# Fewer slots for expert weights, and residual rows that stay in on-chip memory

## The chip, the core and the metric

The kernel runs on one core of a Trainium2 chip. The core has a matrix engine (TensorE, PE in the profile), a vector engine (VectorE, DVE), an activation engine (ScalarE, ACT), GpSimd (POOL) and a sync engine (SyncE, SP) that mainly issues DMAs; 16 DMA engines move data between DRAM and the on-chip memory. The metric is the device time of one execution in microseconds (us), as the median of several runs.

## What is computed

One layer of a decoder: adaLN modulation, a state-space group and an attention group side by side, an output projection, and then a mixture of experts with a shared expert. 1024 prompt tokens and 64 sample tokens are computed together, 1088 rows of 1024 numbers in float32. The change touches only the last part:

```python
def _block(x, c, past, ...):
    ...
    x = x + (gt1[:, None, :] * mix.astype(jnp.float32)).astype(x.dtype)   # residual rows: x1 in the kernel
    h = _norm_modulate(x, g_norm2, sh2, sc2)
    ff = _moe_ffn(h, w_router, router_bias, w_eg, w_eu, w_ed, w_sg, w_su, w_sd)
    x = x + (gt2[:, None, :] * ff.astype(jnp.float32)).astype(x.dtype)    # needs x1 again
    return x, state

def _moe_ffn(...):
    ...  # sigmoid scores, 4 of 8 groups, 6 of 64 experts for each row, weights w
    routed = _grouped_experts(x2, idx, w, w_eg, w_eu, w_ed)   # silu(x@wg) * (x@wu) @ wd, by expert
    shared = _swiglu(x2, w_sg, w_su, w_sd)
    return (routed + shared).reshape(Bn, L, Dm)
```

Each expert has a gate and an up matrix (1024 x 256) and a down matrix (256 x 1024), 1 MB each, and all 64 experts are read once.

## The kernel before

The program is written engine by engine: each engine has its own list of instructions, and semaphores tie them together. Nothing reorders them. The rows are held in nine tiles of 128 rows (the ninth has the 64 sample rows).

**On-chip memory.** Nearly all of it is one array, `arena`, in which each tensor has a fixed place that later tensors reuse. `x1`, the residual rows, lies at 39200 to 48416 (numbers of float32 in each partition). In the routed stage the weights of experts go into rings of slots: `gu_ring` (L337) has `GU_RING` = 6 slots of 2 MB from 4096 on, one for the gate and up matrices of an expert; `down_ring` (L338) has `DOWN_RING` = 5 slots of 1 MB, one at 28672 and four from 39200 on. These four lie over `x1`. That is why SP stores `x1` to a DRAM tensor `x1_tiles` first (`x_tiles` in the profile) and reads it back at the end.

**The shared stage** (about 1224 to 1334 us of the span). For each tile PE computes gate and up of the shared expert (L899, here of the next tile), ACT and POOL make the hidden rows, PE transposes them (L921) and multiplies by the down matrix (L927), ACT evicts the result into one of two buffers `y_buf` (L1944) and SP stores it to `moe_rows` in DRAM. Before an eviction into a buffer, ACT waits until the store from it two tiles ago has landed. The same SP queue holds, ahead of these stores: the rows of `h2`, the two stores of `x1` (L2240, L2241) and one DMA of 5376 KB that fills with zeros the part of `moe_rows` to which routed rows will be added (L2243). Beside this, DVE, PE and POOL compute the routing tables; `table_ready` tells SP that the experts are sorted.

**The routed stage** (about 1341 to 2117 us). The experts are sorted by how many rows they have, and a fixed plan (`ROUNDS`, with `NR` = 62 rounds, then a loop of two more) says which expert's rows stand in which quarter of a block of 128 rows: a large expert takes up to three rounds, and a round can hold the rest of one expert and all of another, or two small ones. For round b, PE does: gate/up of round b + 1 (L1011), transposes of the gathered rows of round b + 2 (L990), down of round b (L1022), transposes of hidden rows (L1029), an index product (L941). POOL gathers the rows of a round from `h2_rows` in DRAM and scatters the results, adding them to `moe_rows`.

**The loads of experts.** SP alone issues them, in a fixed order. `gu_sorted(k)` loads gate and up of the k-th expert of the order; from the seventh on it first waits until PE's gate/up of the last round of expert k - `GU_RING` is done. `down_sorted(k)` does the same for down, with `DOWN_RING`. In the order, gate/up k comes ahead of down k - 1, and an instruction that waits holds up all behind it:

```python
            for k in range(GU_RING, E):
                e_before, e_now = e_now, gu_sorted(k)
                down_sorted(k - 1, e_before)
```

The first loads are issued earlier: two experts' gate/up and one down as soon as `table_ready` is there, the others of the first `GU_RING` after the last shared tile is evicted. After these, and once the stores of shared rows and the zero fill have landed, SP adds one to `shared_stored`; ACT, DVE and POOL wait for it before round 0. The last round of each expert, in the plan's order, is 0, 1, 4, 4, 5, 5, 6, 7, 8, 9, 10, 10, 11, 12, 14, 14, 16, 16, 17, 17 for experts 0 to 19; expert 10 and 11 start in round 10, experts 18 and 19 in round 17, 38 and 39 in round 36, 58 and 59 in round 55.

**The end** (about 2124 us on). SP loads for each tile the shared rows, `x1` and the routed rows (L2306 to L2308); DVE adds the two (L1691), multiplies by the gate (L1692), adds to `x1` (L1693), and after the norm applies the modulation (L1703, L1704); SP stores the result.

Of the kernel before, what the change touches and what calls it, by code (L numbers as in the profile page):

```python
# [31 lines left out]
P = 128  # L32
D = 1024
# [31 lines left out]
MAXPAIR = (T * TOPK // P + E + 1) // 2  # L65
GU_RING = 6
DOWN_RING = 5
MAXBLK = 128
# [9 lines left out]
def rows(t):  # L78
    return P if t < 8 else NS
# [83 lines left out]
def hymba_program(nc, ap, out):  # L163

    ctx = ExitStack()
    with ctx:
# [6 lines left out]
        h2_dram = nc.dram_tensor("h2_rows", (T, D), F32, kind="Internal").ap()  # L173
        x1_dram = nc.dram_tensor("x1_tiles", (P, NT * D), F32, kind="Internal").ap()
        y_dram = nc.dram_tensor("moe_rows", (2 * (T + P), D), F32, kind="Internal").ap()
# [161 lines left out]
        gu_ring = arena(4096, GU_RING, 2, KD * FE)  # L337
        down_ring = [arena(28672, 2 * D)] + [arena(39200 + 2 * D * i, 2 * D) for i in range(DOWN_RING - 1)]  # L338
        x_rows = arena(0, 2, D)
# [727 lines left out]
        def _(dve):  # L1067
# [619 lines left out]
            for t in range(NT + 2):  # L1687
                if t < NT:
                    m, s_ = rows(t), int(t == 8)
                    dve.wait_ge(ld_y[t], 48)  # L1690
                    dlink(tt(y_rows[0:m, t, :], y_rows[0:m, t, :], y_rows2[t][0:m, :], ALU.add))  # L1691
                    dlink(tt(y_rows[0:m, t, :], y_rows[0:m, t, :], fin_rows[0:m, s_, :], ALU.mult))  # L1692
                    tt(x1[0:m, t, :], x1[0:m, t, :], y_rows[0:m, t, :], ALU.add).then_inc(x2_ready, 1)  # L1693
                if 1 <= t <= NT:
                    m = rows(t - 1)
                    dve.wait_ge(x2_sq, t)
                    ts(ssq[0:m, t - 1:t], ssq[0:m, t - 1:t], 1.0 / D, EPS, ALU.mult, ALU.add).then_inc(x_var, 1)
                if t >= 2:
                    i = t - 2
                    m, s_ = rows(i), int(i == 8)  # L1700
                    dve.wait_ge(x_std, NT + 3 + i)
                    dlink(dve.reciprocal(rstd[0:m, i:i + 1], rstd[0:m, i:i + 1]))
                    dlink(stt(x1[0:m, i, :], x1[0:m, i, :], rstd[0:m, i:i + 1], fin_rows[0:m, 2 + s_, :], ALU.mult, ALU.mult))  # L1703
                    tt(x1[0:m, i, :], x1[0:m, i, :], fin_rows[0:m, 4 + s_, :], ALU.add).then_inc(y_out_ready, 1)  # L1704
# [396 lines left out]
        def _(sp):  # L2101
# [137 lines left out]
            sp.sem_inc(rows_stored, 1)  # L2239
            dma(x1_dram[:, 0:8 * D], x1[:, 0:8, :].rearrange("p t d -> p (t d)")).then_inc(stored_h2[0], 16)  # L2240
            dma(x1_dram[0:NS, 8 * D:], x1[0:NS, 8, :]).then_inc(stored_h2[0], 16)  # L2241
            sp.wait_ge(routed, 1)
# [28 lines left out]
            slots.wait_full(sp, ("W", NT - 1, 1))  # L2271
            e_before = gu_sorted(0)
            e_now = gu_sorted(1)
            down_sorted(0, e_before)
            t = NT - 1
            sp.wait_ge(ys2_ready, NT)
            store(sp, y_dram[t * P:t * P + rows(t), :], y_buf[0:rows(t), t % 2, :], stored_ys[t % 2])
            sp.wait_ge(xn2_ready, NT)
            sp.wait_ge(stored_h2[0], 112)
            for k in range(2, GU_RING):  # L2280
                e_before, e_now = e_now, gu_sorted(k)
                down_sorted(k - 1, e_before)
            sp.wait_ge(stored_ys[0], 80)
# [21 lines left out]
            for t in range(NT):  # L2305
                dma(y_rows[0:rows(t), t, :], y_dram[t * P:t * P + rows(t), :]).then_inc(ld_y[t], 16)  # L2306
                dma(x1[0:rows(t), t, :], x1_dram[0:rows(t), t * D:(t + 1) * D]).then_inc(ld_y[t], 16)
                dma(y_rows2[t][0:rows(t), :], y_dram[T + P + t * P:T + P + t * P + rows(t), :]).then_inc(ld_y[t], 16)  # L2308
# [37 lines left out]
```

## Time and profile before

| | us |
|---|---|
| median of 3 runs (2194.28 to 2196.66) | 2195.11 |
| the profiled execution | 2194.29 |
| its span | 2192.5 |
| PE busy | 1926.2 |
| DVE busy | 871.3 |
| ACT busy | 470.6 |

The trace is of one execution, and all times in it count from the start of its span; what lies around the span is 1.8 us. A busy time is the time in which an engine ran an instruction; waits of the SP queue are time in which SP could issue no DMA. The DMA share is the mean busy share of the 16 DMA engines; it can come out a little above 1. The time from an issue to the landing runs from the start of the issuing instruction to the last update of the semaphore of that DMA.

### The profile page before, as it was taken

Reading aid. Unit: us, or ns where it says so; the run is one execution under the profiler, and the core shown is the slowest. Engines: PE = TensorE matmul, PEld = TensorE weight load, DVE = VectorE, ACT = ScalarE, POOL = GpSimd, SP = SyncE. Lnnn points to the kernel's source line nnn. Section 1 sums busy time; section 2 is a strip of 40 time slices with the busy share of each in tenths; the row PEclk is TensorE's granted clock in tenths of the full one; section 3 lists DMA queues with packets and bytes.
Section 4 is the critical chain, followed back from the end, with each engine's and each line's share of the span. In section 5 each row is a group of like instructions: output and inputs, shape, how many; then the busy total and the mean of one; then the engine's idle time right before and its main releaser. Section 6 shows DMA issues by size and latency. Waiting matters only on the chain.

```text
span 2192.5 us, 25291 instructions
## 1 busy us (share of the span) xinstructions
PE 1926.2 (88%) x8864; PEld 996.2 (45%) x8864; DVE 871.3 (40%) x2383; ACT 470.6 (21%) x899; POOL 217.6 (10%) x178
## 2 busy tenths in 40 slices
PE   3569899999988888887988888999999999999970
PEld 1146555555446666333546533444444444444440
DVE  4934631101335554222223623334344344443439
ACT  0122101210135454113023211111111111111122
POOL 0000000100000000030000001122221222212110
PEclk8679756899999998999997899999999999999985
DMA  7921001100112000444001628999999999999656
GB/s 282 366 78 44 22 1 51 70 0 1 48 36 79 1 1 20 131 159 144 0 1 48 201 74 332 350 380 375 374 383 371 381 376 360 358 374 383 215 166 237
DMA packets 99946, 398.64 MB, mean 182 GB/s; under 512 B 27055, under 2 KB 29779, under 8 KB 70108
## 3 DMA queue, kind: packets, MB, share of 16 engines
q1 hardware_dynamic: 80812, 327.81, 39.1%
q0 software_dynamic: 19008, 69.21, 12.0%
q8 instruction: 72, 1.18, 0.2%
q14 instruction: 54, 0.44, 0.1%
HBM read 333.88 MB, written 61.52 MB: 180 GB/s over the span
## 4 chain that ended last, share of the span: by engine, by line
PE 45%; issue 5%; DVE 3%; ACT 2%; DMA 1%; POOL 0%; POOLq 0%; SPq 0%; DVEq 0%; ACTq 0%
PE psum L1011 21%; PE psum L1022 10%; PE psum L865 5%; PE psum L990 3%; PE psum L1029 1%; PE psum L844 1%; PE psum L899 1%; PE psum L889 1%; PE psum L906 1%; PE psum L941 1%; DVE arena L1703 1%; DVE arena L1692 1%; DVE arena L1704 1%; DVE arena L1693 1%; DVE arena L1691 0%
## 5 line engine op out<-in xcount | busy, mean ns | idle before, releaser
L1011 PE MATMUL psum<-arena 128*32 128x512 f32 (+2 forms) x2016 | 464.3, 597 | 1.1 <-ACT arena L1957 1.1
L1011 PEld LDWEIGHTS psum<-arena 128*32 128x32 f32 (+2 forms) x2016 | 169.2, 139 | 242.1 <-issue 240.2
L1022 PE MATMUL psum<-arena,tail 128*32 128x512 f32 (+2 forms) x1000 | 231.6, 595 | 0.0
L1642 DVE TENSOR_TENSOR arena<-arena,psum 128x256 f32<-128x256 f32 x65 | 39.6, 610 | 339.9 <-ACT arena L1962 336.9
L2086 POOL DMA_INDIRECT moe_rows<-arena x64 | 101.7, 1589 | 575.6 <-DVE arena L1670 439.5
L1022 PEld LDWEIGHTS psum<-arena,tail 128*32 128x32 f32 (+2 forms) x1000 | 79.9, 138 | 105.3 <-issue 105.3
L713 PE MATMUL psum<-arena 128*128 128x512 f32 (+1 forms) x384 | 126.5, 493 | 0.0
L865 PE MATMUL psum<-arena 128*128 128x512 f32 (+1 forms) x288 | 124.3, 593 | 0.8 <-ACT arena L1888 0.5
L1962 ACT ACTIVATE arena<-psum 128x256 f32<-128x256 f32 x65 | 25.0, 384 | 444.9 <-PE psum L1011 444.9
L754 PE MATMUL psum<-arena 128*128 128x512 f32 (+2 forms) x192 | 86.8, 568 | 10.4 <-ACT arena L1818 10.4
L865 PEld LDWEIGHTS psum<-arena 128*128 128x128 f32 (+1 forms) x288 | 68.5, 239 | 55.3 <-issue 40.1
L713 PEld LDWEIGHTS psum<-arena 128*128 128x128 f32 x384 | 63.8, 193 | 62.6 <-issue 62.6
L573 PE MATMUL psum<-arena 128*32 128x512 f32 x256 | 50.5, 931 | 44.2 <-DMA arena<-in_w_ada 33.5
L1609 DVE TENSOR_TENSOR arena<-tail,arena 128x1152 bf16<-128x1152 f32 (+3 forms) x89 | 85.3, 984 | 0.0
L990 PEld LDWEIGHTS psum<-tail,arena 128*128 128x128 f32 x528 | 60.2, 142 | 49.7 <-issue 41.3
L1976 ACT ACTIVATE arena<-psum,arena 128x512 f32<-128x512 f32 x64 | 44.0, 687 | 159.0 <-PE psum L1022 148.9
L1670 DVE TENSOR_SCALAR arena<-psum,arena 128x512 f32<-128x512 f32 x64 | 48.0, 751 | 74.6 <-PE psum L1022 74.6
L763 PE MATMUL psum<-arena 128*128 128x64 f32 x576 | 77.0, 283 | 0.0
L1957 ACT ACTIVATE arena<-psum 128x1024 f32<-128x1024 f32 x66 | 67.6, 1024 | 42.5 <-PE psum L990 42.5
L990 PE MATMUL psum<-tail,arena 128*128 128x128 f32 x528 | 70.9, 278 | 6.4 <-DMA arena<-h_rows,arena 6.4
L763 PEld LDWEIGHTS psum<-arena 128*128 128x128 f32 x576 | 75.2, 206 | 0.0
L2074 POOL DMA_INDIRECT arena<-h_rows,arena x68 | 67.2, 988 | 48.1 <-DVE arena L1635 24.7
(481 smaller groups left out, 2440.6 us busy)
## 6 DMA issues: line engine op xcount, KB each, us to landing
arena<-in_w_exp_gate SPq DMA_DIRECT2D x66, 1024.0 KB, 20.1
arena<-in_w_exp_up SPq DMA_DIRECT2D x66, 1024.0 KB, 25.1
arena<-in_w_exp_down SPq DMA_DIRECT2D x66, 1024.0 KB, 22.5
arena<-in_w_ada SPq DMA_DIRECT2D x12, 2048.0 KB, 8.3
arena<-in_w_ada_final SPq DMA_DIRECT2D x4, 2048.0 KB, 8.8
arena<-in_cache_k SPq DMA_DIRECT2D x32, 256.0 KB, 3.9
arena<-in_cache_v SPq DMA_DIRECT2D x32, 256.0 KB, 3.0
arena<-moe_rows SPq DMA_DIRECT2D x16, 512.0 KB, 12.7
```

What stands on the lines that cost most here:

```text
L573: ins = pe.matmul(slot[2 + g % 2][32 * j:32 * (j + 1), :], cs_t[:, k, :], ada_w[:, n % 2, k % KPER, j * 512:(j + 1) * 512], start=(k == 0) ...
L713: ins = pe.matmul(slot[b][:, 0:c1 - c0], w_q[:, k, w * DA + j * P:w * DA + (j + 1) * P], hT[:, k, c0:c1], start=(k == 0), stop=(k == KD - 1))
L754: ins = pe.matmul(slot[it % 2][:, c0:c1], qT[:, h, i * P:(i + 1) * P], kT[:, h // 2, c0:c1], start=True, stop=True)
L763: ins = pe.matmul(slot[4 + it % 2][:, 0:DH], pt[:, it % 2, j * P:(j + 1) * P], v[:, j, h * DH:(h + 1) * DH], start=(j == 0), stop=(j == i))
L865: ins = pe.matmul(slot[half][0:rows(t), n * 512:(n + 1) * 512], lhs, w_out[:, half * KA + k, n * 512:(n + 1) * 512], start=(k == 0), stop= ...
L990: ins = pe.transpose(slot[0][:, k * P:(k + 1) * P], x_rows[:, par, k * P:(k + 1) * P], ident)
L1011: ins = pe.matmul(slot[2 + par][lo:hi, :].rearrange("p (u n) -> p u n", u=2), xTs[:, par, k, lo:hi], gu, start=(k == 0), stop=(k == KD - 1))
L1022: ins = pe.matmul(slot[1][lo:hi, n * 512:(n + 1) * 512], hTs[:, k, lo:hi], down_ring[at][:, k * D + n * 512:k * D + (n + 1) * 512], start= ...
L1609: ins = tt(onehot[:, par, :, lo * LANE:hi * LANE], iota_row[:, lo * LANE:hi * LANE].unsqueeze(1).to_broadcast([P, NT, w]), blk_rank[:, par ...
L1957: f(xTs[:, par].rearrange("p k c -> p (k c)"), slot[0], ACT.Copy).then_inc(xt_copied, 1)
L2074: pool.indirect_dma_start(x_rows[:, par, :], None, h2_dram, bass.IndirectOffsetOnAxis(ap=g_idx[:, par:par + 1], axis=0)).then_inc(gathered ...
L2086: pool.indirect_dma_start(y_dram, bass.IndirectOffsetOnAxis(ap=s_idx[:, par:par + 1], axis=0), y_buf[:, par, :], None, compute_op=ALU.add) ...
```

## The change

The rings get 5 and 3 slots. All of them now lie between 4096 and 30720 of `arena`: five gate/up slots up to 24576, and three down slots behind them. `x1` is overlaid by nothing from then on, so the DRAM tensor, its two stores and its nine loads are gone, and so is the wait for the stores. Of the early loads only gate/up and down of the first expert remain ahead of the last shared store, since the next slot lies over the shared weights. The order of the loads behind stays gate/up k, down k - 1.

```diff
@@ -63,8 +63,8 @@
 NEG = -1e30
 MAGIC = 12582912.0
 MAXPAIR = (T * TOPK // P + E + 1) // 2
-GU_RING = 6
-DOWN_RING = 5
+GU_RING = 5
+DOWN_RING = 3
 MAXBLK = 128
 LANE = 32
 CAPS = (10, 9, 9, 8, 8, 7) + (6,) * 5 + (5,) * 11 + (4,) * 8 + (3,) * 16 + (2,) * 14 + (1,) * 4
@@ -171,7 +171,6 @@
         tail_t = ctx.enter_context(nc.sbuf_tensor("tail", [P, 4280], F32))
         psum = ctx.enter_context(nc.psum_tensor("psum", [P, 8, 512], F32))
         h2_dram = nc.dram_tensor("h2_rows", (T, D), F32, kind="Internal").ap()
-        x1_dram = nc.dram_tensor("x1_tiles", (P, NT * D), F32, kind="Internal").ap()
         y_dram = nc.dram_tensor("moe_rows", (2 * (T + P), D), F32, kind="Internal").ap()
 
         def arena(at, *shape, dt=F32, parts=P):
@@ -335,7 +334,7 @@
         sh_gu = arena(13056, KD, 2 * FE)
         sh_d = arena(17152, 2, D)
         gu_ring = arena(4096, GU_RING, 2, KD * FE)
-        down_ring = [arena(28672, 2 * D)] + [arena(39200 + 2 * D * i, 2 * D) for i in range(DOWN_RING - 1)]
+        down_ring = [arena(4096 + 2 * D * (11 + i), 2 * D) for i in (1, 0)] + [arena(4096 + 2 * D * 10, 2 * D)]
         x_rows = arena(0, 2, D)
         xTs = arena(2048, 2, KD, P)
         y_buf = arena(31776, 2, D)
@@ -1687,7 +1686,7 @@
             for t in range(NT + 2):
                 if t < NT:
                     m, s_ = rows(t), int(t == 8)
-                    dve.wait_ge(ld_y[t], 48)
+                    dve.wait_ge(ld_y[t], 32)
                     dlink(tt(y_rows[0:m, t, :], y_rows[0:m, t, :], y_rows2[t][0:m, :], ALU.add))
                     dlink(tt(y_rows[0:m, t, :], y_rows[0:m, t, :], fin_rows[0:m, s_, :], ALU.mult))
                     tt(x1[0:m, t, :], x1[0:m, t, :], y_rows[0:m, t, :], ALU.add).then_inc(x2_ready, 1)
@@ -2237,8 +2236,6 @@
             sp.wait_ge(stored_h2[0], 80)
             sp.wait_ge(stored_h2[1], 64)
             sp.sem_inc(rows_stored, 1)
-            dma(x1_dram[:, 0:8 * D], x1[:, 0:8, :].rearrange("p t d -> p (t d)")).then_inc(stored_h2[0], 16)
-            dma(x1_dram[0:NS, 8 * D:], x1[0:NS, 8, :]).then_inc(stored_h2[0], 16)
             sp.wait_ge(routed, 1)
             dma(y_dram[T:, :].rearrange("(a p) d -> p a d", p=E), y_zero[0:E, :].unsqueeze(1).to_broadcast([E, (T + 2 * P) // E, D])).then_inc(stored_h2[1], 16)
             for t in range(NT - 1):
@@ -2269,17 +2266,16 @@
 
             sp.wait_ge(table_ready, 1)
             slots.wait_full(sp, ("W", NT - 1, 1))
-            e_before = gu_sorted(0)
-            e_now = gu_sorted(1)
-            down_sorted(0, e_before)
+            e_now = gu_sorted(0)
+            down_sorted(0, e_now)
             t = NT - 1
             sp.wait_ge(ys2_ready, NT)
             store(sp, y_dram[t * P:t * P + rows(t), :], y_buf[0:rows(t), t % 2, :], stored_ys[t % 2])
             sp.wait_ge(xn2_ready, NT)
-            sp.wait_ge(stored_h2[0], 112)
-            for k in range(2, GU_RING):
+            for k in range(1, GU_RING):
                 e_before, e_now = e_now, gu_sorted(k)
-                down_sorted(k - 1, e_before)
+                if k > 1:
+                    down_sorted(k - 1, e_before)
             sp.wait_ge(stored_ys[0], 80)
             sp.wait_ge(stored_ys[1], 64)
             sp.wait_ge(stored_h2[1], 80)
@@ -2304,7 +2300,6 @@
             sp.wait_ge(routed_done, 1)
             for t in range(NT):
                 dma(y_rows[0:rows(t), t, :], y_dram[t * P:t * P + rows(t), :]).then_inc(ld_y[t], 16)
-                dma(x1[0:rows(t), t, :], x1_dram[0:rows(t), t * D:(t + 1) * D]).then_inc(ld_y[t], 16)
                 dma(y_rows2[t][0:rows(t), :], y_dram[T + P + t * P:T + P + t * P + rows(t), :]).then_inc(ld_y[t], 16)
             for t in range(NT):
                 sp.wait_ge(y_out_ready, t + 1)
```

On SP, the queue of DMAs, the part from the stores of `h2` rows to the first expert loads stood so before (`x_tiles` and `moe_rows` are the DRAM tensors, `in_w_exp_gate`, `in_w_exp_up` and `in_w_exp_down` the weights):

```order
L518 DMA h_rows<-arena 64x1024 [waits h2_ready]
L2240 DMA x_tiles<-arena 128x8192 [waits stored_h20,stored_h21]
L2241 DMA x_tiles<-arena 64x1024
L2243 DMA moe_rows<-arena 64x21x1024 [waits routed]
L518 DMA moe_rows<-arena 128x1024 [waits ys2_ready] x8
L2259 TENSOR_LOAD arena [waits slot_filled1,table_ready]
```

And now:

```order
L517 DMA h_rows<-arena 64x1024 [waits h2_ready]
L2240 DMA moe_rows<-arena 64x21x1024 [waits stored_h20,stored_h21,routed]
L517 DMA moe_rows<-arena 128x1024 [waits ys2_ready] x8
L2256 TENSOR_LOAD arena [waits slot_filled1,table_ready]
L2256 ISA x2
```

The two stores of `x1` have gone from ahead of the zero fill, and so the fill and the shared stores each stand two DMAs earlier.

Later on the same queue, before, the place of the first wait for a slot: the loads of gate/up 5 and down 4, then those of gate/up 6 and down 5.

```order
L2253 DMA arena<-in_w_exp_up 128x2048
L2256 DMA arena<-in_w_exp_down 128x2048
L2259 TENSOR_LOAD arena [waits stored_h21,stored_ys0,stored_ys1]
L2259 ISA x2
L2253 ISA [waits gu_done]
L2253 DMA arena<-in_w_exp_gate 128x2048
L2253 DMA arena<-in_w_exp_up 128x2048
L2256 DMA arena<-in_w_exp_down 128x2048 [waits down_done]
```

And now, the loads of gate/up 4 and down 3, then those of gate/up 5 and down 4:

```order
L2250 DMA arena<-in_w_exp_up 128x2048
L2253 DMA arena<-in_w_exp_down 128x2048 [waits down_done]
L2256 TENSOR_LOAD arena [waits stored_h21,stored_ys0,stored_ys1]
L2256 ISA x2
L2250 ISA [waits gu_done]
L2250 DMA arena<-in_w_exp_gate 128x2048
L2250 DMA arena<-in_w_exp_up 128x2048
L2253 DMA arena<-in_w_exp_down 128x2048 [waits down_done]
```

The first wait for `down_done` now stands ahead of the waits for the stores and thus ahead of `shared_stored`, which is raised right after them; before it came behind.

## Rows read from the trace of the kernel before

**Rows 1.** The page, part 1: busy time, share of span, instructions by engine.
```profile
PE 1926.2 (88%) x8864; PEld 996.2 (45%) x8864; DVE 871.3 (40%) x2383; ACT 470.6 (21%) x899; POOL 217.6 (10%) x178
```

**Rows 2.** Table of stretches: length, busy time by engine, clock granted, DMA share, GB/s.
```profile
1265.80:1276.00 10.20, 4.73 (x7) 2.14 (x8) 0.00 (x0) 2.18 (x4) 0.73 (x1) 0.50 0.31 127
1267.00:1327.00 60.00, 52.67 (x190) 23.12 (x190) 18.56 (x81) 12.38 (x23) 3.69 (x5) 0.93 0.12 49
1346.00:1366.00 20.00, 19.53 (x75) 9.82 (x74) 7.53 (x26) 3.44 (x5) 0.94 (x1) 0.96 1.01 426
1413.00:2035.00 622.00, 622.00 (x3585) 270.12 (x3582) 255.31 (x937) 109.42 (x157) 133.78 (x104) 1.00 1.02 372
2132.00:2190.00 58.00, 0.00 (x0) 0.00 (x0) 55.93 (x63) 12.68 (x28) 0.00 (x0) 0.51 0.67 260
```

**Rows 3.** Waits of the SP queue from 1200 us on: total us, times, longest.
```profile
SPq L2256 <- PE psum L1022: 423.4, 35, 16.3
```

**Rows 4.** DMA issues of 1226.6 and 1227.5: KB, us to landing; SP's row.
```profile
x_tiles<-arena SPq DMA_DIRECT2D x1, 4096.0 KB, 11.9
...
moe_rows<-arena SPq DMA_DIRECT2D x1, 5376.0 KB, 39.1
...
1227.50 1.35 SPq L2243 DMA_DIRECT2D moe_rows<-arena  x1
```

**Rows 5.** Timeline of ACT, evictions of shared rows: start, us, idle before and releaser.
```profile
1244.87 1.02 ACT L1944 ACTIVATE arena<-psum 128x1024 f32<-128x1024 f32 x1 [3.79 <-PE psum L927]
...
1267.94 1.02 ACT L1944 ACTIVATE arena<-psum 128x1024 f32<-128x1024 f32 x1 [15.61 <-DMA moe_rows<-arena]
```

**Rows 6.** Timeline of PE, fourth and fifth shared tile.
```profile
1252.39 3.70 PE L927 MATMUL psum<-arena,tail 128*128 128x512 f32 x8 [0.47 <-ACT tail L1940]
1255.92 7.03 PE L899 MATMUL psum<-arena 128*128 128x512 f32 x16
...
1270.79 0.69 PE L921 MATMUL psum<-tail,arena 128*128 128x128 f32 x2 [7.84 <-POOL arena L2063]
1271.95 5.69 PE L927 MATMUL psum<-arena,tail 128*128 128x512 f32 x8 [0.47 <-ACT tail L1940]
```

**Rows 7.** Timeline of DVE at the end; DMA issues of 2124.3 and 2124.8 us.
```profile
2131.77 1.23 DVE L1691 TENSOR_TENSOR arena<-arena 128x1024 f32<-128x1024 f32 x1 [11.54 <-DMA arena<-moe_rows]
...
arena<-x_tiles SPq DMA_DIRECT2D x1, 512.0 KB, 5.4
...
arena<-moe_rows SPq DMA_DIRECT2D x1, 512.0 KB, 6.9
```

**Rows 8.** Timelines of SP, ACT and PE around round 0 of the loop.
```profile
1365.37 0.33 SPq L2256 DMA_DIRECT2D arena<-in_w_exp_down  x1
...
1361.94 1.02 ACT L1957 ACTIVATE arena<-psum 128x1024 f32<-128x1024 f32 x1 [0.44 <-PE psum L990]
...
1353.90 7.13 PE L1011 MATMUL psum<-arena 128*128 128x512 f32 x16 [0.24 <-ACT arena L1957]
...
1365.62 7.11 PE L1011 MATMUL psum<-arena 128*128 128x512 f32 x16
```

**Rows 9.** Timeline of PE: down of rounds 4, 5; gate/up of 10, 17.
```profile
1409.02 3.64 PE L1022 MATMUL psum<-arena,tail 128*32 128x512 f32 x32
...
1421.01 3.64 PE L1022 MATMUL psum<-arena,tail 128*32 128x512 f32 x32
...
1460.28 7.07 PE L1011 MATMUL psum<-arena 128*32 128x512 f32 x64
...
1543.34 7.07 PE L1011 MATMUL psum<-arena 128*32 128x512 f32 x64
```

**Rows 10.** DMA issues of 1412.7, 1426.2 and 1498.7: KB, us to landing.
```profile
arena<-in_w_exp_down SPq DMA_DIRECT2D x1, 1024.0 KB, 5.7
...
arena<-in_w_exp_up SPq DMA_DIRECT2D x1, 1024.0 KB, 24.0
...
arena<-in_w_exp_up SPq DMA_DIRECT2D x1, 1024.0 KB, 39.2
```

## The prediction

> **What bounds the kernel now.** I read the page first: PE is busy 88% of the span, DVE 40% [rows 1]. Then the table of stretches, because an average says nothing of where a change acts. From 1413 to 2035 us PE is busy 622.00 of 622.00 us at the full clock (2.4 GHz), and in the same stretch the DMA share is 1.02, that is full, at 372 GB/s [rows 2]. So in the routed stage PE sets the pace and the DMA engines keep up with nothing to spare: the weights arrive just as fast as PE eats them, and what keeps PE from feeling it is the stock of weights in the slots. The waits of the SP queue say how that stock is kept: it stood 423.4 us for a down slot to come free [rows 3]. SP wants to run ahead and the slots hold it. The change takes slots away, so the question is how much stock each round needs. The other two places that the change touches are the shared stage, where PE once stands idle, and the end, where DVE waits for its first rows; both are read below.
>
> The profiled execution took 2194.29 us, 1.8 us more than its span of 2192.5; the median of the three runs is 2195.11, 0.8 above it. I sum on 2194.29 and add the 0.8 at the end. About 0.2% (4.4 us) is what a measurement of this kernel can tell from no change.
>
> **Part 1, the store of the residual rows goes.** At 1226.6 SP issues 4 MB of x1, and at 1227.50 the zero fill of `moe_rows` behind it; they land 11.9 and 39.1 us after their issues, at 1238.5 and 1266.6 [rows 4]. The fill alone thus takes 28.1 us. The first store of shared rows is behind the fill, and ACT waits for it 15.61 us until 1267.94 [rows 5]. ACT's lateness reaches PE: PE ends the gate/up of the next tile at 1255.92 + 7.03 = 1262.95, and starts the next transposes at 1270.79 after 7.84 us of idle time. The matmuls behind it take 5.69 us where the same eight took 3.70 one tile earlier [rows 6], since after that idle time the granted clock is 0.50 (1.2 GHz) [rows 2]. Cost of the wait: 7.84 + 1.99 = 9.8 us. Without the x1 store the fill lands at about 1226.6 + 28.1 = 1255, the store behind it by 1257; a plain tile later than ACT's eviction at 1244.87, that is at about 1256, ACT wants it. Its remaining wait of 1 us ends before PE is done at 1262.95. So the wait goes: **-9.8 us** (bounds -8 and -10). Next late is nothing on DMA's side: the stores of the following tiles find empty queues (DMA share 0.12 from 1267 on [rows 2]).
>
> **Part 2, the reload at the end goes.** DVE's first add waits for the three loads of tile 0 until 2131.77 [rows 7]. Those of x1 and of the second half of `moe_rows` were issued 0.5 us apart and land 5.4 and 6.9 us after their issues, so without the x1 load the last lands about one such transfer earlier, 1.5 to 2.0 us. Afterwards DVE is busy, 55.93 of 58 us [rows 2], either way. **-1.7 us.** The other 8 x1 loads are hidden behind DVE now and give nothing.
>
> **Part 3, the signal that opens the loop.** Before, SP issued five down loads without any wait and then set `shared_stored`. Now the fourth down load waits for the down matmuls of round 0, and the signal stands behind it on SP; ACT, DVE and POOL all wait for that signal before their first round. In the trace the sixth down load waits for those matmuls and is issued at 1365.37, ACT evicts the turned rows of round 2 from 1361.94 for 1.02 us and PE starts that gate/up at 1365.62 [rows 8]. In the changed kernel ACT can start its gate only after 1365.37 + 0.33 and some semaphore steps, at about 1366.3, its eviction 0.8 us later ends at 1368.1 and PE starts at about 1368.5: **+2.9 us**, once (bounds 0 and 4). The second gate/up load, which now waits for the last shared rows, is wanted only at 1353.90, after the first gate/up [rows 8]; I take no cost for it (0 to 2).
>
> **Part 4, the stock of weights.** SP's order is gate/up k+1, down k, gate/up k+2, down k+1. A down load k now waits until expert k-3 is done (k-5 before), and each gate/up load stands behind the down load ahead of it on the queue. Expert 2 has three rounds and is done with the down matmuls of round 4, at 1409.02 + 3.64 = 1412.66 [rows 9]. In the trace the load that waits for this is down 7, issued at 1412.7, and it lands 5.7 us later, which is what one load costs in a short queue [rows 10]. After the change it is down 5. So from this moment the same queue is behind by down 5, gate/up 7, down 6, gate/up 8: 6 MB.
>
> What a MB costs in the full queue: the up load of expert 11 is issued at 1426.2 and lands 24.0 us later, at 1450.2; that of expert 19 at 1498.7 + 39.2 = 1537.9 [rows 10]. Between lie 8 experts of 3 MB: 87.7 / 24 = 3.65 us each. 6 MB are then 21.9 us. With weights alone in the queues, at 426 GB/s from 1346 to 1366 [rows 2], a MB takes 1.049 / 426 = 2.46 us, and 6 MB 14.8. How much the stock covers: expert 11 is wanted at 1460.28, 10.1 us after it landed; expert 19 at 1543.34, 5.4 us after [rows 9]. So PE loses 21.9 - 10.1 = 11.8 us by expert 11 and 21.9 - 5.4 = 16.5 us by expert 19, at the price of the full queue; 14.8 - 5.4 = 9.4 at that of weights alone. While PE stands, fewer scatters and gathers run beside the weights, so I take a value between, nearer the full queue's: **+13 us**.
>
> Later the stock can't grow again as it did. From the rounds, ten gate/up loads (experts 7, 19, 29, 31, 39, 41, 49, 51, 59, 61) get their slot only one round before PE wants them; with five down slots none did. In that round one down and two gate/up loads, 3 MB, must land. A round is 1421.01 - 1409.02 = 12.0 us [rows 9]. The fixed part of a load is 5.7 - 2.46 = 3.2 us; 3 MB take 3 x 3.65 + 3.2 = 14.2 us in the full queue (2.2 us late) and 3 x 2.46 + 3.2 = 10.6 alone (in time). Two of the ten are in the 13 us; the other eight cost 0 to 17.6 us, and as a scatter and a gather run in every round I take 1.5 each: **+12 us**.
>
> A rule of the Trainium skill speaks against this loss: "Trainium Kernel Development and Optimization", section Best Practices, says to double-buffer so that DMA overlaps with compute, and three slots are more than two. By that rule part 4 would be 0 and the sum -6.6 in place of +18.4; with the DMA share at 1.02 [rows 2] there is nothing left to overlap with, so I take it for the first rival only. For the transfers, "DMA: Bandwidth & Descriptors" (section Anatomy of one DMA, the path of DMAs that GpSimd issues) has a fit of 2.0 us plus bytes / 436 GB/s; by it, as an estimate, 3 MB in a row are 9.2 us and the eight loads cost nothing.
>
> **Clock.** After an idle time of 7.84 us the clock fell and cost 2 us (part 1). The waits of rounds 10, 17 and of two or three later ones may be of 4 us and more, so up to 10 us; but where the queue is the limit, a slower PE only waits less for the next load. **+2 us** (0 to 8).
>
> **Sum:** -9.8 - 1.7 + 2.9 + 13 + 12 + 2 = +18.4. 2194.29 + 18.4 + 0.8 = 2213.5 us.
>
> **Rivals.** (A) *Faster.* The loss of part 4 stays hidden, and the gains of parts 1 and 2 come through with the cost of part 3: 2195.1 - 9.8 - 1.7 + 2.9 = 2186.5. For it: both loads that I followed landed 5.4 us or more before use, and PE never waited. It decides if the queue catches up 6 MB within the 47.6 us from 1412.66 to 1460.28, which needs a MB at under 3.0 us there (15 MB and the fixed part), against the 3.65 seen. I give it 0.11. It is also what double-buffering as the Trainium skill has it (page and section above) would lead one to expect. (B) *No change.* Part 4 stays at its low end, 9.4 and nothing later, and the clock costs nothing: 2195.1 - 8.6 + 9.4 = 2195.9, within the noise: 0.09. (C) *Worse.* Six down loads (5, 19, 29, 39, 49, 59) get their slot only when the round before their own is done, and are wanted at 1421.01 - 1412.66 = 8.4 us after [rows 9]; alone one takes 5.7, behind 3 MB of backlog 4 x 3.65 + 3.2 = 17.8, that is 9.4 us late. If the backlog is there each time, four of them beyond what is counted add 38: 2251. Against it: the load ahead of them was issued two rounds earlier. 0.06. That the change doesn't do what it says I exclude: the order of the built program has no row of `x_tiles` left.
>
> **How the numbers follow.** The forecast, slower, has 0.74. Its own range is part 4 from 12 to 34, the rest from -9 to +3 (part 3 at 4 and the clock at 8): 2198 to 2232. The 8-in-10 range goes down to 2195, so that B is in it, and up to 2238, where the clock's 8 us are in it too: A below and C above are left out, 0.17. Faster by more than 0.2%: case A, 0.11. Same: case B, 0.09. Slower: the forecast and C, 0.80.
>
> **What would show it.** Part 1: no idle time of PE before the transposes of the fourth shared tile, and the routed stage starting some 10 us earlier. Part 2: DVE's first add 1.5 to 2 us sooner after SP's first load. Part 3: PE's third gate/up of the loop waits 3 us. Part 4: PE rows of gate/up (`L1011`'s line) with idle time ended by DMA from the weights, the longest at rounds 10 and 17, then small ones at 27, 29, 36, 38, 46, 48, 55, 57, and none on the down side; the DMA share below 1 near 1400. I am wrong if PE waits for no weights, or waits for the down weights, or if the shared stage still stands at the fill.

## The result, and the profile after

The changed kernel takes **2227.61 us** (median of four runs, 2224.8 to 2229.44), the kernel before 2195.89 beside it (four runs, 2194.28 to 2197.43). The ratio is 1.0143, 95% interval 1.0126 to 1.0161: 31.7 us slower. The forecast was slower, 2213.5, with a range of 2195 to 2238. The profiled execution has a span of 2227.7 us, 35.2 more than before.

The page of the changed kernel first: busy time by engine (as in [rows 1]), the chain of work that ended last by engine and by line (cut by the page itself), and the group of the gate/up matmuls, now `L1010` (lines of the changed kernel are one lower there).

```profile
PE 1935.7 (87%) x8864; PEld 995.0 (45%) x8864; DVE 870.8 (39%) x2383; ACT 469.7 (21%) x899; POOL 217.3 (10%) x178
...
PE 37%; DMA 9%; issue 5%; DVE 3%; ACT 2%; SPq 1%; POOL 0%; POOLq 0%; DVEq 0%; ACTq 0%
PE psum L1010 17%; DMA arena<-in_w_exp_up 8%; PE psum L1021 8%; PE psum L864 5%; PE psum L989 2%; PE psum L898 1%; PE psum L888 1%; PE psum L905 1%; DVE arena L1702 1%; PE psum L892 1%; DVE arena L1691 0%; DVE arena L1692 0%; DVE arena L170
...
L1010 PE MATMUL psum<-arena 128*32 128x512 f32 (+2 forms) x2016 | 474.8, 608 | 32.3 <-DMA arena<-in_w_exp_up 31.2
```

PE now stands 32.3 us ahead of the gate/up matmuls, 31.2 of them for the up half of the weights, and this transfer holds 8% of the chain. The same group in the kernel before, with 1.1 us:

```profile
L1011 PE MATMUL psum<-arena 128*32 128x512 f32 (+2 forms) x2016 | 464.3, 597 | 1.1 <-ACT arena L1957 1.1
```

Next the table of stretches, with the columns of [rows 2]: the stretch that [rows 2] has, and one ahead of the loop's longest wait.

```profile
1413.00:2035.00 622.00, 591.74 (x3397) 258.09 (x3397) 240.49 (x884) 102.59 (x147) 126.00 (x99) 0.98 0.98 353
...
1380.00:1410.00 30.00, 30.00 (x237) 12.48 (x236) 12.85 (x41) 6.28 (x9) 5.14 (x4) 1.00 0.58 143
```

The second of these stretches in the kernel before:

```profile
1380.00:1410.00 30.00, 30.00 (x213) 12.76 (x215) 10.55 (x36) 5.45 (x8) 6.46 (x6) 1.00 1.03 375
```

From 1413 to 2035 PE was busy all of the time before [rows 2] and is idle for 30 us of it now; the DMA share went from 1.02 to 0.98. So PE and DMA both lost. From 1380 to 1410 the DMA engines are 0.58 busy in place of 1.03, while PE works on without a pause. The waits of the SP queue say why (total, times, longest), against 423.4 us, 35 times, at most 16.3 in [rows 3]:

```profile
SPq L2253 <- PE psum L1021: 635.7, 36, 33.7
```

`L2253` is the down load. The view has no wait of `L2250`, the gate/up load, for its own slot: when SP gets to a gate/up load, the slot has always been free for some time. The profile before had 120.0 us of such waits in 19 pieces, so there SP did stand at the gate/up slots now and then:

```profile
SPq L2253 <- PE psum L1011: 120.0, 19, 18.2
```

PE's timeline, the gate/up matmuls that had to wait, with those of an undisturbed round ahead; the bracket is the idle time before:

```profile
1660.60 7.07 PE L1010 MATMUL psum<-arena 128*32 128x512 f32 x64
...
1466.93 8.40 PE L1010 MATMUL psum<-arena 128*32 128x512 f32 x64 [8.83 <-DMA arena<-in_w_exp_up]
...
1676.44 9.47 PE L1010 MATMUL psum<-arena 128*64 128x512 f32 x32 [3.88 <-DMA arena<-in_w_exp_up]
...
1792.03 9.70 PE L1010 MATMUL psum<-arena 128*64 128x512 f32 x32 [3.87 <-DMA arena<-in_w_exp_up]
```

And the stretches around the start of round 10's matmuls:

```profile
1463.00:1469.50 6.50, 2.56 (x13) 0.71 (x17) 0.00 (x0) 0.00 (x0) 0.00 (x0) 0.50 1.04 340
1470.00:1475.00 5.00, 5.00 (x52) 1.46 (x44) 0.00 (x0) 0.00 (x0) 0.00 (x0) 1.00 1.02 423
```

These are rounds 10, 27 and 36. Each of these three waits is paid twice: the idle time, and then matmuls of 8.4 to 9.7 us in place of 7.1, since the granted clock is 0.50 (1.2 GHz) behind the wait and 1.00 (2.4 GHz) again some us later. Most of the shorter waits are paid once: behind 1.7 us at rounds 7 and 17 and 2.5 us at round 46 the matmuls take 7.1.

A late load need not have idle DMA engines ahead of it. Ahead of round 27 they are full, though SP issues nothing from 1641.2 to 1660.1:

```profile
1642.00:1661.00 19.00, 19.00 (x118) 8.63 (x114) 8.24 (x27) 4.19 (x6) 2.57 (x2) 1.00 1.02 351
```

**Where the 35.2 us are.** I cut the span at PE's first transpose of the normalised rows (`L906` before, `L905` now; 18.7 us ahead of the shared expert's first gate/up), at the start of the first gate/up of round 0 (1341.94 before, 1334.35 now) and at the end of the last down matmuls of all 64 rounds (2115.72 and 2152.75).

| stretch | before, us | after, us | difference |
|---|---|---|---|
| ahead of the first cut (noise) | 1152.4 | 1154.9 | +2.5 |
| norm and shared stage, to the gate/up of round 0 | 189.6 | 179.4 | -10.1 |
| routed stage | 773.8 | 818.4 | +44.6 |
| end | 76.8 | 75.0 | -1.8 |

In the routed stage, summed by round over the time from the end of the down matmuls to the next gate/up beyond its usual 0.35 us: round 2 1.8; rounds 7, 10 and 17 12.6; fourteen late rounds in all 34.7, of which 20.3 from round 27 on. Five slow gate/ups behind them (rounds 2, 10, 27, 36 and 55, at 8.4 to 9.7 against 7.1) add 10.5. 34.7 + 10.5 = 45.2, against 44.6 seen. Counted from start to start of the gate/ups, which needs no usual value, the waits are 34.1, and the sum is 44.6.

### The profile page after: what moved, and what is told of

It reads as the page before. It is cut to its first block, busy times and chain, and to the rows that moved or that the text cites. A ratio compares the mean times of both kernels' runs of the same rounds, so it can differ in the third digit from the quotient of the medians.

```text
span 2227.7 us, 25279 instructions
## 1 busy us (share of the span) xinstructions
PE 1935.7 (87%) x8864; PEld 995.0 (45%) x8864; DVE 870.8 (39%) x2383; ACT 469.7 (21%) x899; POOL 217.3 (10%) x178
## 3 DMA queue, kind: packets, MB, share of 16 engines
q0 software_dynamic: 19008, 69.21, 11.9%
## 4 chain that ended last, share of the span: by engine, by line
PE 37%; DMA 9%; issue 5%; DVE 3%; ACT 2%; SPq 1%; POOL 0%; POOLq 0%; DVEq 0%; ACTq 0%
PE psum L1010 17%; DMA arena<-in_w_exp_up 8%; PE psum L1021 8%; PE psum L864 5%; PE psum L989 2%; PE psum L898 1%; PE psum L888 1%; PE psum L905 1%; DVE arena L1702 1%; PE psum L892 1%; DVE arena L1691 0%; DVE arena L1692 0%; DVE arena L1703 0%; PE psum L843 0%; DVE arena L1690 0%
## 5 line engine op out<-in xcount | busy, mean ns | idle before, releaser
L1010 PE MATMUL psum<-arena 128*32 128x512 f32 (+2 forms) x2016 | 474.8, 608 | 32.3 <-DMA arena<-in_w_exp_up 31.2
L1010 PEld LDWEIGHTS psum<-arena 128*32 128x32 f32 (+2 forms) x2016 | 175.3, 141 | 278.5 <-issue 276.9
```

The lines of the kernel that those rows point to most:

```text
L1010: ins = pe.matmul(slot[2 + par][lo:hi, :].rearrange("p (u n) -> p u n", u=2), xTs[:, par, k, lo:hi], gu, start=(k == 0), stop=(k == KD - 1))
```

## The experiments

Two things were in question. My forecast said "stock", without saying of which slots. The trace puts the waits at the gate/up weights. So: do five gate/up slots cost the time, or three down slots? And if the down slots, is it the storage, or the order of the loads on SP's one queue?

**Three down slots alone, in the kernel before.**

```diff
-DOWN_RING = 5
+DOWN_RING = 3
-            for k in range(2, GU_RING):
+            for k in range(2, 4):
...
-            for k in range(GU_RING, E):
+            for k in range(4, E):
```

> The kernel before (six gate/up slots, residual rows still stored and read back) with three down slots alone; shared_stored is raised right before the first down load that has to wait, two loads earlier than in the kernel before. Theory of the down slots (the gate/up load of expert k+1 stands on SP's queue behind the down load of k, which waits for the down slot of k-3, so that its own free slot helps nothing): gate/up late at rounds 10, 27, 36, 46 and 55 as in the changed kernel, some 30 us late in all and 10 us more of slow clock, 2195.9 + 30 to 42 = 2226 to 2238 us. Rival of the gate/up slots (the waits stand at the gate/up weights, so the fifth slot in place of the sixth costs the time): no late load, 2194 to 2198 us. Middle, both: 2205 to 2220 us.

2237.18 us, ratio 1.0179 (1.0150 to 1.0208). Its gate/up group and SP's wait, as above:

```profile
L1011 PE MATMUL psum<-arena 128*32 128x512 f32 (+2 forms) x2016 | 470.1, 605 | 32.0 <-DMA arena<-in_w_exp_up 30.9
...
SPq L2256 <- PE psum L1022: 624.3, 36, 33.6
```

The expectation of the down slots is met, in time and in the late rounds. With six gate/up slots and as much idle time for late weights as in the changed kernel (32.0 and 32.3 us), the sixth gate/up slot helps nothing. The loss is that of the down slots, though PE waits for gate/up weights.

**Five gate/up slots alone, in the kernel before.**

```diff
-GU_RING = 6
+GU_RING = 5
...
-        gu_ring = arena(4096, GU_RING, 2, KD * FE)
+        gu_ring = arena(8192, GU_RING, 2, KD * FE)
```

> The kernel before with five gate/up slots alone (five down slots, residual rows stored and read back as before). Theory of the down slots: no gate/up waits for its weights by more than 1 us in the routed stage, 2194 to 2199 us. Rival of the gate/up slots: late loads at rounds 10, 27, 36 and 55 and 2220 us or more.

2198.03 us, ratio 0.9997 (0.9978 to 1.0016). PE is busy throughout, as before the change:

```profile
1413.00:2035.00 622.00, 622.00 (x3602) 269.37 (x3601) 255.34 (x936) 109.59 (x157) 133.56 (x104) 1.00 1.02 373
```

The rival of the gate/up slots falls: taken alone, the sixth slot is worth nothing that can be measured.

**The same bytes, given out as four gate/up and five down slots, in the changed kernel.**

```diff
-GU_RING = 5
-DOWN_RING = 3
+GU_RING = 4
+DOWN_RING = 5
...
-        gu_ring = arena(4096, GU_RING, 2, KD * FE)
-        down_ring = [arena(4096 + 2 * D * (11 + i), 2 * D) for i in (1, 0)] + [arena(4096 + 2 * D * 10, 2 * D)]
+        gu_ring = arena(12288, GU_RING, 2, KD * FE)
+        down_ring = [arena(28672, 2 * D)] + [arena(4096 + 2 * D * i, 2 * D) for i in range(4)]
```

> The changed kernel with its 13 half slots given out as four gate/up and five down slots in place of five and three: the same bytes on chip, one gate/up slot less. Theory of the down slots: the late loads of rounds 27 to 57 are gone and those of rounds 10 and 17 halve, because the down load no longer stands in front of the gate/up load; 13 us of lateness at most is left of 34.7, so 2227.6 - 20 to - 38 = 2190 to 2208 us. Rival of the gate/up slots: one slot less makes every wait longer, 2235 to 2270 us. Rival that all the stock counts alike (13 half slots is what matters): 2222 to 2233 us.

2192.91 us, ratio 0.9975 (0.9961 to 0.9988). One wait for weights is left, at round 10, and SP now waits for gate/up slots and hardly for down slots:

```profile
PE psum L1010 <- DMA arena<-in_w_exp_up: 3.7, 1, 3.7
...
SPq L2250 <- PE psum L1010: 519.3, 35, 33.2
SPq L2253 <- PE psum L1021: 50.0, 12, 11.2
```

It is not the total of the stock that counts: the same 13 half slots, shared out another way, are better than five and three by 1.7% of the time, 37 us.

**The same slots, another order on SP.** The down load of expert k-2, in place of k-1, stands behind the gate/up load of k.

```diff
...
-                e_before, e_now = e_now, gu_sorted(k)
-                down_sorted(k - 1, e_before)
-            down_sorted(E - 1, e_now)
+                es.append(gu_sorted(k))
+                down_sorted(k - 2, es[k - 2])
+            for k in (E - 2, E - 1):
+                down_sorted(k, es[k])
```

> The changed kernel with another order on SP's queue and the same slots: the down load of expert k-2 stands behind the gate/up load of k, in place of that of k-1 (shared_stored is raised before the first down load that waits, since only three of them come before it now). Theory of the order (a gate/up load whose slot is free waits behind a down load whose slot is not): the gate/up waits go, a few down loads come some us late (the one at round 10 most), 10 us or less of lateness in place of 34.7 and little slow clock, 2227.6 - 25 to - 38 = 2190 to 2203 us. Rival of the storage (three down slots hold too little, in whatever order): the lateness moves to the down weights, 2220 to 2235 us. Rival of the gate/up slots: the order on the queue counts little, 2222 to 2230 us.

2198.81 us, ratio 1.0001 (0.9985 to 1.0016): 1.4% of the time by the order (and the earlier signal that comes with it, worth nothing measurable by itself, below; in the traces the routed stage is 784.9 us here and 811.9 with the early signal alone). One example of what the order does is expert 29. First the changed kernel, PE's and SP's timelines: the gate/up that frees the slot, the down matmuls that the load ahead of it on SP waits for, and the loads.

```profile
1636.72 7.07 PE L1010 MATMUL psum<-arena 128*32 128x512 f32 x64
...
1656.46 3.64 PE L1021 MATMUL psum<-arena,tail 128*32 128x512 f32 x32
...
1660.16 0.33 SPq L2253 DMA_DIRECT2D arena<-in_w_exp_down  x1
1661.24 0.34 SPq L2250 DMA_DIRECT2D arena<-in_w_exp_gate  x1
1661.68 0.43 SPq L2250 DMA_DIRECT2D arena<-in_w_exp_up  x1
```

The same in this kernel, with the gate/up that uses the weights at the end:

```profile
1630.92 7.08 PE L1010 MATMUL psum<-arena 128*32 128x512 f32 x64
...
1638.20 0.34 SPq L2250 DMA_DIRECT2D arena<-in_w_exp_gate  x1
...
1666.69 7.09 PE L1010 MATMUL psum<-arena 128*64 128x512 f32 x32
```

In the changed kernel the slot is free at 1636.72 + 7.07 = 1643.8, but the load ahead of it on SP waits for the down matmuls that end at 1656.46 + 3.64 = 1660.1, and the gate/up load follows 1.1 us later: 17.4 us lost with a free slot. Here it is issued 0.2 us after its slot is free (1638.0). Over all gate/up loads that need a slot to come free (59, in the kernel before 58), the mean from the slot's release to the issue is 19.6 us in the changed kernel (none under 14.7), 9.5 in this one and 9.2 in the kernel before.

The example is the rule. In the change's order gate/up k stands behind down k-2, and that load waits, with three slots, for the down matmuls of expert k-5: each of the 59 loads is issued 1.1 to 4.4 us after these end. With six gate/up slots it stands behind the same matmuls, which is why the sixth slot helped nothing. The other order, or a fourth down slot, puts the matmuls of expert k-6 there. The loss goes with the time from the issue to the use, and not with the time that a slot stands free (in the mean 31.3 us with three down slots alone, at about the same loss, and 2.4 with five gate/up slots alone, against 9.2 before, at none). The shortest time from the issue of an up load to PE's want of it is 33.9 us in the kernel before and 27.9 with five gate/up slots alone, 22.2 in this run, 16.2 with four and five slots, and 10.6 in the changed kernel and with three down slots alone.

What stays here is 8.0 us of waits for down weights, since a down load still waits for the expert three before it, the longest at round 10:

```profile
PE psum L1021 <- DMA arena<-in_w_exp_down: 8.0, 3, 6.1
PE psum L1010 <- DMA arena<-in_w_exp_up: 0.7, 1, 0.7
```

**Four down slots, in either order.** A fourth slot in two halves, where the zeros and the dead tables of the routing lay; first with the order of the last experiment, then with that of the changed kernel (there with the early signal of the experiment after next). The diff is cut to the ring; the down load and the down matmuls address the slot in two halves.

```diff
...
-DOWN_RING = 3
+DOWN_RING = 4
-        down_ring = [arena(4096 + 2 * D * (11 + i), 2 * D) for i in (1, 0)] + [arena(4096 + 2 * D * 10, 2 * D)]
+        down_ring = [arena(4096 + 2 * D * (12 - i), 2, D) for i in range(3)] + [arena(30720, 2, 6496)[:, :, 0:D]]
...
```

> The changed kernel with the order of the run before (the down load of expert k-2 behind the gate/up load of k) and a fourth down slot, in two halves that lie where the zeros of the zero fill and the dead tables of the routing were. Theory: the order and the fourth slot leave no load late by more than 1.5 us, the routed stage is as long as before the change (774 to 778 us), the gains of the shared stage and of the end stay: 8 to 11.5 us less than before, ratio 0.9948 to 0.9963. Rival (the queue is full, and any lost slot costs): down of round 10 and the like still late by 3 us or more and a slow gate/up behind it, ratio 0.998 to 1.003. Rival (loads in two halves are slower): the down loads take longer by 1 us or more each, ratio 1.0 or more.

> The changed kernel in its own order (the down load of expert k-1 behind the gate/up load of k) with the fourth down slot in two halves and shared_stored raised before the down load of expert 3; with the run before it, it makes a square of three or four down slots in either order. Theory (one more down slot lets the down load at the head of SP's queue go a round or so earlier, and so takes most of what the order costs): one or two gate/up loads late, at round 10 or 17, by 3 to 7 us in all with a slow gate/up behind them, none at rounds 27 to 58; 4 us less than before to 2 us more, ratio 0.998 to 1.001. Rival (the fourth slot is worth little without the other order): late loads at rounds 27 to 58 as in the changed kernel, ratio 1.008 to 1.014.

2187.55 us, ratio 0.9964 (0.9948 to 0.9980), and 2192.66 us, ratio 0.9986 (0.9973 to 1.0000). All that PE waited for weights in the one and in the other:

```profile
PE psum L1021 <- DMA arena<-in_w_exp_down: 3.6, 1, 3.6
```

```profile
PE psum L1010 <- DMA arena<-in_w_exp_up: 5.6, 2, 4.3
```

The square of ratios: three down slots 1.0143 in the change's order and 1.0001 in the other, four 0.9986 and 0.9964. Either the order or one more down slot takes most of the loss away; together they add little. In the traces the routed stage is 44.6 us longer than before with neither, 11.1 with the other order, 7.1 with the fourth slot and 4.1 with both. The second expectation was met (two late gate/ups, rounds 10 and 17). The first was not quite: the down of round 17 was late by 3.6 us where I had asked for under 1.5, with slow matmuls behind it as its first rival has them (5.34 us in place of 3.64), and the ratio lies just outside what I gave, and below the rivals'. The one with both is faster than the kernel before, by 7.9 us.

**The gains alone: the kernel before without the store and the reload of the residual rows** (this part of the computation is left out: the last addition reads weights in place of these rows).

```diff
...
-            dma(x1_dram[:, 0:8 * D], x1[:, 0:8, :].rearrange("p t d -> p (t d)")).then_inc(stored_h2[0], 16)
-            dma(x1_dram[0:NS, 8 * D:], x1[0:NS, 8, :]).then_inc(stored_h2[0], 16)
...
-                dma(x1[0:rows(t), t, :], x1_dram[0:rows(t), t * D:(t + 1) * D]).then_inc(ld_y[t], 16)
```

> The kernel before with six gate/up and five down slots, without the store of the residual rows and without reading them back; the down slots lie over these rows as before, so the last addition reads weights in their place and y_prompt and y_sample carry that: this part of the computation is left out. It is the first two terms of the forecast alone. Theory: 9.8 us less in the shared stage and 1.7 us less at the end, ratio 0.9948 (11.5 of 2195), no late weights. Rival (the store is hidden, and its place is taken by the zero fill's transfer or by the second load): ratio 0.998 to 1.000.

2184.74 us, ratio 0.9952 (0.9931 to 0.9974): 10.5 us by the ratio, of the 11.5 forecast; the interval is 5.7 to 15.2 us. The rival (hidden store) falls.

**The signal earlier, in the changed kernel.**

```diff
-            for k in range(1, GU_RING):
+            for k in range(1, GU_RING - 1):
...
+            e_before, e_now = e_now, gu_sorted(GU_RING - 1)
             sp.wait_ge(stored_ys[0], 80)
             sp.wait_ge(stored_ys[1], 64)
             sp.wait_ge(stored_h2[1], 80)
             sp.sem_inc(shared_stored, 1)
+            down_sorted(GU_RING - 2, e_before)
```

> The changed kernel with shared_stored raised before the down load of expert 3 in place of behind it. Theory (the signal stood behind that load's wait for down of round 0): the gate/up of round 2 is no longer late (1.8 us) and runs at full clock (8.8 to 7.1 us), ScalarE's and VectorE's waits for that signal (12.0 and 7.8 us) shrink to a few; 2 to 3.5 us less, ratio 1.0130 to 1.0135 to the kernel before in place of 1.0143; the later late loads stay. Rival (the time is given back at the next late load, since the rounds run ahead of the queue that sets them): round 2 is on time, but the lateness at rounds 7 and 10 grows by as much, ratio 1.014 to 1.015.

2226.61 us, ratio 1.0144 (1.0120 to 1.0167): no difference to the changed kernel that this measurement can tell. ACT's third gate, in the changed kernel and in this one, and PE's gate/up of round 2 in both:

```profile
1358.20 0.38 ACT L1961 ACTIVATE arena<-psum 128x256 f32<-128x256 f32 x1 [12.02 <-SPq L2282]
...
1359.84 8.81 PE L1010 MATMUL psum<-arena 128*128 128x512 f32 x16
```

```profile
1352.15 0.38 ACT L1961 ACTIVATE arena<-psum 128x256 f32<-128x256 f32 x1 [7.27 <-PE psum L1010]
...
1356.66 7.11 PE L1010 MATMUL psum<-arena 128*128 128x512 f32 x16
```

The wait and the slow clock are gone, as the theory has it, and PE's wait for weights is 29.5 us in all (31.2 in the changed kernel). The ratio is where the rival put it. But its sign did not come: rounds 7 and 10 are late by 10.7 us together in both kernels. Whether those 3.5 us reach the end is **not settled**: the interval is 10 us wide.

**Half of each down load left out, in the changed kernel** (2.5 MB an expert in place of 3; the second half of each down matrix is left out).

```diff
-                dma(down_ring[q], ed[bass.ds(e, 1)].rearrange("a p n -> (a p) n")).then_inc(ld_down[q], 16)
+                dma(down_ring[q][:, 0:D], ed[bass.ds(e, 1)].rearrange("a p n -> (a p) n")[:, 0:D]).then_inc(ld_down[q], 16)
```

> The changed kernel with half of each down load left out (the second 1024 of 2048 numbers of each partition are never read from DRAM, so the experts' outputs are wrong): the same slots, waits and order, but 2.5 MB in place of 3 MB for an expert. Theory (where an expert has one round only, 3 MB do not fit in 12 us of a full queue, so bytes set the late loads behind the release): the lateness of rounds 27 to 58 falls from 20.3 to under 8 us, that of rounds 10 and 17 from 10.7 to under 4 us, and the time by 18 to 35 us, ratio 0.998 to 1.006. Rival (the order on the queue alone sets them: a gate/up load is issued 17 us after its slot is free, whatever the bytes): lateness of 16 us or more at rounds 27 to 58, ratio 1.009 to 1.014.

2201.47 us, ratio 1.0024 (1.0005 to 1.0043). The stretch of [rows 2], and PE's waits:

```profile
1413.00:2035.00 622.00, 607.71 (x3506) 266.97 (x3504) 247.43 (x906) 106.60 (x153) 128.95 (x101) 1.00 0.93 317
```

```profile
PE psum L1010 <- DMA arena<-in_w_exp_up: 15.4, 11, 2.4
...
SPq L2253 <- PE psum L1021: 599.8, 36, 33.7
```

The time fits the theory of the bytes, the lateness neither: the rounds from 27 on are late by 11.9 us together (20.3 with all bytes; I had set under 8 for the one, 16 or more for the other), rounds 10 and 17 by 3.1 (10.7). So both act. With the DMA share at 0.93 and SP waiting as long as before, eight rounds from 27 on are still late by 1.1 to 2.4 us each: that I put down to the order, since their loads are issued a round before use whatever they weigh (at least 10.6 us before PE wants them, as in the changed kernel). The rest, 8.4 us there and 7.6 at rounds 10 and 17, is bytes. It is more than one trace differs from another: from start to start of the gate/ups the rounds from 27 on are late by 11.2 us here, and by 19.8, 19.3 and 17.4 in the changed kernel, with three down slots alone and with the early signal.

## Why the forecast was right in sign and 14 us short

- **Part 1 (forecast -9.8):** -10.1 in the trace. PE's transposes, `L921` in [rows 6], have no idle time any more, and ACT's wait of 15.61 us [rows 5] is 5.13, hidden from PE as forecast (at most other tiles ACT waits 3.79 for PE itself). The timelines of PE and ACT:

```profile
1265.26 0.38 PE L920 MATMUL psum<-tail,arena 128*128 128x128 f32 x2
...
1259.93 1.02 ACT L1943 ACTIVATE arena<-psum 128x1024 f32<-128x1024 f32 x1 [5.13 <-DMA moe_rows<-arena]
```

- **Part 2 (-1.7):** -1.8. DVE's first add starts 5.7 us after SP's first load, against 7.9 before (the add in [rows 7]); first the load before, then the load and the add now:

```profile
2123.90 0.33 SPq L2306 DMA_DIRECT2D arena<-moe_rows  x1
...
2161.26 0.33 SPq L2302 DMA_DIRECT2D arena<-moe_rows  x1
...
2166.98 1.23 DVE L1690 TENSOR_TENSOR arena<-arena 128x1024 f32<-128x1024 f32 x1 [9.73 <-ACTq L1990]
```

- **Part 3 (+2.9):** the place was right, ACT's bracket above names the signal; 1.8 us late and 1.7 of slow clock, 3.5. I had not priced the clock there.
- **Part 4, first term (+13):** rounds 7, 10 and 17 are 12.6 us late. The missing queue time is directly to be seen: 30 us at 0.58 in place of 1.03 from 1380 to 1410 are 13.5 us in which the DMA engines had nothing, from 1392.1 on with two gate/up slots free. I called it a stock that is 6 MB short; it is idle DMA time behind a load that may not go yet. That 13 came so near is in part luck: I chose it between two prices, 9.4 and 16.5. And I had named rounds 10 and 17 as the longest waits: round 17 has 1.7 us, and rounds 27, 36 and 55 have 3.9 to 4.4.
- **Part 4, second term (+12):** this step is mis-sized; 20.3 us, beyond my own bound of 17.6 (1.1 of them at rounds 39 and 58, which I had not named). The ten loads that I counted are the right ones: their up halves are issued 10.6 to 11.0 us before PE wants them, those before 34.7 to 57.8. The sum let each of the eight rounds start with an empty queue and 3 MB. Take expert 29: its up load, issued at 1661.68, lands 14.6 us later, at 1676.3, and PE wanted it at about 1672.5. But the up load of expert 28, issued at 1640.74, takes 24.3 us and is still on its way until 1665.0. The DMA issues of 1661.68 and 1640.74, KB and us to landing:

```profile
arena<-in_w_exp_up SPq DMA_DIRECT2D x1, 1024.0 KB, 14.6
...
arena<-in_w_exp_up SPq DMA_DIRECT2D x1, 1024.0 KB, 24.3
```

So 3 MB and what was left of an older load went through in 1676.3 - 1660.2 = 16.1 us, where I had 14.2 at most; the other price that I named for 3 MB in a row, 9.2, fell further short. The late rounds come in pairs two rounds apart (27 and 29, 36 and 38, 46 and 48, 55 and 57); the first of each pair carry 15.0 of the 20.3 us, the other six rounds about 1 us each. With less in the queue (half the down bytes) the eight become alike, at 1.1 to 2.4 us: the 1.5 that I took for each is what the order costs without a backlog, as far as that run shows it.
- **Clock (+2):** the step that failed. I let a slow PE be made up for, because "a slower PE only waits less for the next load". It cost 10.5 us, 8.8 without the 1.7 of round 2, over my bound of 8 either way, and the books close only if all of it stays (45.2 summed, 44.6 seen). The next load here waits for a slot that the slow matmuls themselves free, so it moves back with them; this reason fits the waits of SP, and no run tests it alone.
- **The rivals:** A fell by the first late row, and B by the time and the late rows after round 10. C fell as well: no down load was late. I put that down to the gate/up load that stands behind each and is late first. That the down loads come late instead shows only with the other order (6.1 us at round 10).
- **The rule of double-buffering** ("Trainium Kernel Development and Optimization" in the Trainium skill, Best Practices), by which part 4 would have been 0: with three slots the trace has 635.7 us of SP's waits and 31.2 of PE's. A count of slots above two did not decide it; the same three slots make the routed stage 44.6 us longer or 11.1, by the order of the loads behind them.

Terms against trace: -10.1 - 1.8 + 3.5 + 12.6 + 20.3 + 8.8 (the clock without round 2's) = +33.3 where I had +18.4; with 2.5 us of noise ahead of the change that is 35.8, and the span grew by 35.2.

## What to carry to other kernels

When one queue issues the loads of two rings, its order is worth as much as its storage: look for loads that are issued long after their own slot is free and shortly before their use, since the ring that PE waits for need not be the one that is short. The sign is that the waits of the queue are all at the other ring's line; here the late loads went out 10.6 to 11.0 us before their use, where it was 34.7 or more. A DMA share below 1 need not come with it: it was 0.58 ahead of round 10, but 1.02 ahead of round 27. Before taking slots away, follow which release each load stands behind, and put ahead on the queue what is released first; and price the slow clock behind the longer waits. Here those of 3.9 to 8.8 us had it, at 1.3 to 2.6 us each, and all of it stayed in the sum.

## What the runs showed that I had not expected

The shared stage comes in two lengths in kernels that do the same in it. Of the kernels without the store of x1, three took 174.2 to 174.7 us and four more, beside the changed kernel, 178.8 to 179.6 (cut as in the table). The difference arises ahead of the routing; the same 65 us from the first cut on, with four gate/up and five down slots (of the longer kind) and with the other order and three down slots (of the shorter), columns as above:

```profile
1163.40:1228.40 65.00, 53.50 (x286) 44.63 (x287) 23.49 (x75) 25.37 (x24) 0.00 (x0) 0.79 0.14 57
```

```profile
1162.50:1227.50 65.00, 52.04 (x318) 42.84 (x319) 25.66 (x81) 27.46 (x26) 0.00 (x0) 0.87 0.16 65
```

The mean granted clock is 0.79 in the one and 0.87 in the other. Both have idle times of 1.3 to 1.7 us ahead of each tile from 39 us on; in the changed kernel, which is of the longer kind, the clock falls to 0.50 four times between 41 and 69 us, in the one of the shorter kind once between 39 and 67. Why the one or the other comes, no run tells. The kernel before is of the longer kind too, so the -10.1 of part 1 compares like with like; whether a kernel with the store ever has the shorter, its three traces (187.1 to 189.6 us) do not tell:

```profile
1152.40:1217.40 65.00, 53.36 (x286) 44.47 (x286) 23.45 (x75) 25.32 (x24) 0.00 (x0) 0.79 0.14 57
```

About 5 us come and go this way, more than some of the effects that were sought here.
